# Expert weights in pairs: full-precision matmuls on column tiles, 2 MB loads for two experts

## What is computed

```
def _expert_choice_moe(xn, w_router, w_gate, w_up, w_down):
    cap = EC_FACTOR * n_tok // N_EXPERTS           # 64 latent, 16 context
    aff = jax.nn.softmax(jnp.dot(xt, w_router), axis=-1)
    g, idx = lax.top_k(aff.T, cap)
    xe = xt[idx]
    h = jax.nn.silu(einsum('ecd,edf->ecf', xe, w_gate)) * einsum('ecd,edf->ecf', xe, w_up)
    ye = einsum('ecf,efd->ecd', h, w_down) * g[..., None]
    out = jnp.zeros_like(xt).at[idx.reshape(-1)].add(ye.reshape(-1, D))
```

## Time and profile before

| | us |
|---|---|
| median of three runs | 2026.26 |
| profiled execution | 2036.07 |
| its span, first to last instruction | 2034.3 |
| PE busy | 1811.8 (89%) |
| VectorE busy | 1511.7 (74%) |
| ScalarE busy | 1144.3 (56%) |
| GpSimd busy | 527.7 (26%) |
| weight loads busy (PEld) | 1273.2 (63%) |

### The profile page before, as it was taken

The page is one execution under the profiler, slowest core; times in us unless marked ns, Lnnn a source line. Parts: engine busy times, 40 slices in busy tenths (PEclk is TensorE's granted clock), DMA queues, the critical chain, the costliest instruction groups (busy, mean ns, idle before and its releaser), DMA issues.

```text
span 2034.3 us, 24624 instructions
## 1 busy us (share of the span) xinstructions
PE 1811.8 (89%) x8919; PEld 1273.2 (63%) x8919; DVE 1511.7 (74%) x1438; ACT 1144.3 (56%) x1134; POOL 527.7 (26%) x320
## 2 busy tenths in 40 slices
PE   5899789699999999999478799898699999999995
PEld 2788567366666666665257588777466666666663
DVE  2477553599999999998255466635799999999994
ACT  2477621277777777775231235412477777777773
POOL 1223210214343433331210320000123334343332
PEclk8899887699999999999788779796799999999997
DMA  9300726699999999999730510007499999999992
GB/s 387 104 1 1 279 104 234 259 347 379 382 367 380 364 383 368 380 387 345 96 131 1 191 63 2 1 1 303 159 362 374 379 383 368 380 368 383 366 387 61
DMA packets 139901, 519.03 MB, mean 255 GB/s; under 512 B 14943, under 2 KB 15231, under 8 KB 138814
## 3 DMA queue, kind: packets, MB, share of 16 engines
q1 hardware_dynamic: 131248, 488.02, 62.7%
q0 software_dynamic: 7216, 24.79, 6.3%
q10 hardware_dynamic: 1374, 5.37, 0.6%
HBM read 496.90 MB, written 21.24 MB: 255 GB/s over the span
## 4 chain that ended last, share of the span: by engine, by line
PE 65%; DVE 15%; issue 7%; ACT 6%; DMA 4%; SPq 1%; POOL 1%; DVEq 0%; POOLq 0%; ACTq 0%
PE ps L783 25%; PE ps L788 14%; DVE whl L1536 7%; PE ps L739 6%; PE ps L988 4%; ACT whl L1158 3%; PE ps L1035 2%; DMA ring<-in_at_w_qkv 2%; PE ps L1008 2%; PE ps L1024 2%; DMA ring<-in_mod_w 2%; PE ps L719 1%; DVE W L1554 1%; PE ps L892 1%; SPq L353 1%
## 5 line engine op out<-in xcount | busy, mean ns | idle before, releaser
L1536 DVE TENSOR_TENSOR whl<-ring,whl 128x2048 fp32r<-128x2048 f32 x384 | 922.8, 2428 | 84.8 <-ACT whl L1158 81.6
L1158 ACT ACTIVATE whl<-ring 128x2048 fp32r<-128x2048 f32 x384 | 735.8, 1917 | 247.4 <-PE ps L788 247.1
L783 PE MATMUL ps<-whl,xs_hl 128*80 128x512 f32 x2048 | 558.8, 395 | 8.3 <-DVE xs_hl L1560 4.8
L783 PEld LDWEIGHTS ps<-whl,xs_hl 128*80 128x80 f32 x2048 | 299.5, 149 | 168.0 <-issue 7.0
L788 PE MATMUL ps<-whl,xs_hl 128*80 128x512 f32 x1024 | 322.4, 396 | 19.0 <-DVE whl L1536 19.0
L783 PE MATMUL ps<-whl,hs_hl 128*80 128x512 f32 x1024 | 280.8, 396 | 3.4 <-ACT hs_hl L1065 3.4
L788 PEld LDWEIGHTS ps<-whl,xs_hl 128*80 128x80 f32 x1024 | 147.7, 148 | 117.4 <-DVE whl L1536 41.9
L580 POOL TENSOR_TENSOR W<-W 80x1024 f32<-80x1024 f32 x32 | 89.9, 2808 | 495.5 <-ACT W L1196 495.5
L783 PEld LDWEIGHTS ps<-whl,hs_hl 128*80 128x80 f32 x1024 | 153.3, 150 | 89.1 <-ACT hs_hl L1065 3.6
L788 PE MATMUL ps<-whl,hs_hl 128*80 128x512 f32 x512 | 160.8, 396 | 0.0
L574 POOL COPY sg<-g_t 80x1 f32 (+1 forms) x32 | 82.7, 2585 | 189.8 <-DMA x_mid<-W,si 99.1
(11 more groups left out here) (253 smaller groups left out, 2481.9 us busy)
## 6 DMA issues: line engine op xcount, KB each, us to landing
ring<-in_moe_w_gate SPq DMA_DIRECT2D x128, 1024.0 KB, 8.0
ring<-in_moe_w_up SPq DMA_DIRECT2D x128, 1024.0 KB, 7.2
ring<-in_moe_w_down SPq DMA_DIRECT2D x128, 1024.0 KB, 7.2
ring<-in_mod_w SPq DMA_DIRECT2D x48, 1024.0 KB, 9.8
ring<-in_rg_w_in SPq DMA_DIRECT2D x8, 1024.0 KB, 21.9
ring<-in_at_w_qkv SPq DMA_DIRECT2D x8, 768.0 KB, 20.3
x_hat<-r ACTq DMA_DIRECT2D x2, 2560.0 KB, 19.0
ring<-in_rg_w_out SPq DMA_DIRECT2D x4, 1024.0 KB, 9.6
```

Source lines behind the costliest of these rows:

```text
L783: nc.tensor.matmul(ps[0:CE, bank + n, :], xhl[:, part, k, :], w[:, 0, n * 512:(n + 1) * 512], start=(k == 0 and part == 0), stop=False)
L1158: nc.scalar.activation(whl[:, whl_slot(u), 0, :], ring[:, slot, :], ACT.Copy).then_inc(whi_ok, 1)
L1536: v.tensor_tensor(whl[:, whl_slot(u), 1, :], ring[:, n % MSLOTS, :], whl[:, whl_slot(u), 0, :].bitcast(F32), ALU.subtract).then_inc(wlo_ok, 1)
```

## The change

- Experts are worked on in pairs (8 pairs in a layer). No weight is split: the matmuls take float32 operands. For a contraction block and a half of the columns, expert a's 64 latent rows are the stationary operand of a matmul into PSUM partitions 64a to 64a+63, so that the two experts stand on two column tiles; the 16 context rows of two experts and two halves are four matmuls into partitions 0, 32, 64 and 96.
- All 12 slots hold raw weights. The host lays the weights out so that one load of 2 MB brings two contraction blocks of both experts into two neighbouring slots, with 16 KB of one piece for each partition. A load waits for the matmuls that used its slots (`moe_used`).
- x of a pair is gathered by two indirect DMAs (128 latent rows, 48 rows with the context's), turned and modulated in two parts; scale and shift are taken from the mod vectors by broadcast. The router's indices and weights are kept in pair form (ten small copies).
- VectorE alone forms the output (one operation for 128 latent rows, four for the context), and GpSimd scatters in two rounds of two DMAs, the second behind the landing of the first.
- `mod_w`, `rg_w_out` and `at_w_o` are laid out by the host with 8 KB of one piece per partition and slot; gains, rotary table and sinks come ready from the host in 3 loads instead of 5.
- Half of the qkv loads go out behind mod vectors 9 and 10 as slots come free, the other half when vector 10 has been used; none waits for `x_mid`. The first four blocks are split before it.

The core of the diff:

```diff
+                def part(slot, w, i, s):
+                    sp.dma_start(ring[:, slot:slot + 2, :].rearrange("p (o a) n -> p o (a n)", o=1),
+                                 w3[w][:, bass.ds(i * 4 + s, 1), :]).then_inc(slot_ready[slot], 16)
...
+                def step_loads(i, par, more, _):
+                    for n in range(0, 24 if more else 8, 2):
+                        what = n // 8 if more else 1
+                        sp.wait_ge(moe_used, i * PAIR_USES + (LAYER_USES * layer + n // 2 + 3))
+                        part(n % SLOTS, (0, 2, 1)[what], i + int(what != 1), n % 8 // 2)
...
+            load_mod(9, moe_used, lambda s: LAYER_USES - 6 + s // 2 + 1)
+            load_mod(10, moe_used, lambda s: LAYER_USES - 4 + s // 2 + 1)
...
+            for s in range(4, KB):
+                sp.wait_ge(moe_used, LAYER_USES - 4 + s // 2 + 1)
+                load_qkv(s)
+            for s in range(4):
+                sp.wait_ge(ring_used, used(10, s))
+                load_qkv(s)
...
+                    if rows_left:
+                        next_rows(i + 2)
+                    pool.wait_ge(ob_ok, i * 5 + (41 * layer + 1 + 5))
+                    pool.wait_ge(sg_ok, i * 4 + 4 * (pb + 1))
+                    for a in range(2):
+                        passed()
+                        scatter(si_l[:, a:a + 1], ob_l[a * CL:(a + 1) * CL, :])
+                        scatter(si_c[:, a:a + 1], ob_c[a * CG:a * CG + CC, :])
+                        pool.wait_ge(scattered, i * 64 + (64 * pb + 32 * (a + 1)))
...
+                def product(n0, ready_at, bank, lat, ctx):
+                    for s in range(4):
+                        slots = [(n0 + 2 * s + a) % SLOTS for a in range(2)]
+                        pe.wait_ge(slot_ready[slots[0]], ready_at(n0 + 2 * s))
+                        for h in range(2):
+                            k = 2 * s + h
+                            for n in range(2):
+                                cols = slice(h * D + n * 512, h * D + (n + 1) * 512)
+                                for a in range(2):
+                                    nc.tensor.matmul(ps[a * CL:(a + 1) * CL, bank + n, :], lat(a, k), ring[:, slots[a], cols],
+                                                     start=(k == 0), stop=(k == KB - 1))
+                            for q in range(4):
+                                a, n = q // 2, q % 2
+                                mm = nc.tensor.matmul(ps[q * CG:q * CG + CC, bank + 2, :], ctx(a, k),
+                                                      ring[:, slots[a], h * D + n * 512:h * D + (n + 1) * 512],
+                                                      start=(k == 0), stop=(k == KB - 1))
+                        mm.then_inc(moe_used, 1)
+                        yield s
...
+                    if more:
+                        pe.wait_ge(xt_ok, i * 2 + 2 * (pb + 2))
+                        pe.wait_ge(ob_ok, i * 5 + (41 * layer + 1))
+                        pe.wait_ge(sil_ok, i * 2 + 2 * (pb + 1))
+                        for s in gate_up(0, at, x, 1 - par):
+                            if s < 2:
+                                h_turn(i, s)
...
+                    pe.wait_ge(ht_ok, i * 2 + 2 * (pb + 1))
+                    for s in down(8 if more else 0, at, y):
+                        if s < 3 and rows_left:
+                            x_turn(i + 2, s)
...
+def pair_rows(w):
+    w = slot_rows(w)
+    return w.reshape(2, NP, 2, 4, P, 2 * D).transpose(0, 1, 3, 4, 2, 5).reshape(2, NP * 4, P, 4 * D)
```

More of the change, by code:

```diff
@@ L198, in build @@
         xn2 = work(5 * D, 0)
[L199 to L205, removed]
+        xt = work(2 * KB * XW, 0).rearrange("p (u k n) -> p u k n", u=2, k=KB)
+        ht_l = work(D).rearrange("p (k n) -> p k n", k=KB)
+        ht_c = work(512).rearrange("p (k n) -> p k n", k=4)
+        xg_l = work(D, 5 * D)
+        hs_l = work(D)
+        hs_c = work(512)
+        work(512)
+        xg_c = work(D)
+        ob_l = work(D)
+        ob_c = work(D)
+        gg_l = work(D)
+        gg_c = work(512)
         tk = work(512)
@@ L272, in runs, with loads_before, ready, used @@
             return out
[L277 to L303, removed]
+        def loads_before(name, slot):
+            n = 0
+            for what in SLOT_LOADS[slot // 4]:
+                if what == name:
+                    return n
+                if what in ("moe0", "moe1"):
+                    n += 0 if slot % 2 else SLOT_USES
+                else:
+                    n += 1
+        def ready(name, slot):
+            return 16 * (loads_before(name, slot) + 1)
+        def used(v, s):
+            return 4 * MOD_ORDER.index(v) + s % 4 + 1
+        def first_ready(layer, n):
+            return 16 * (loads_before(f"moe{layer}", n % SLOTS) + (n - 8) // SLOTS + 1)
+        def body_ready(layer, i, n):
+            return i * 32 + 16 * (loads_before(f"moe{layer}", n % SLOTS) + (1 if n % SLOTS < 8 else 2) + n // SLOTS + 1)
         def steps(eng, body):
-            with eng.Fori(0, NE // 2 - 1) as i:
+            with eng.Fori(0, NP // 2 - 1) as j:
                 for par in range(2):
-                    body(i * 2 + par, i, par, True, True)
-            body(NE - 2, NE // 2 - 1, 0, True, False)
-            body(NE - 1, NE // 2 - 1, 1, False, False)
+                    body(j * 2 + par, par, True, True)
+            body(NP - 2, 0, True, False)
+            body(NP - 1, 1, False, False)
         x_tiles = x_all.rearrange("(t p) d -> p t d", p=P)
@@ L355, in pair @@
[L355 to L365, removed]
@@ L367, in load_moe, with put @@
-            def load_moe(layer):
[L368 to L376, removed]
+            def put(slot, src):
+                sp.dma_start(ring[:, slot, :], src).then_inc(slot_ready[slot], 16)
@@ L377, in load_moe @@
                     else:
                         sp.wait_ge(out_mm, 2 * NT)
[L379 to L389, removed]
+                    part(slot, int(n >= 16), 0, n % 8 // 2)
@@ L856, in experts @@
+                at = lambda n: first_ready(layer, n)
+                pe.wait_ge(gg_ok, 2 * (layer + 1))
+                x_turn(0, 0)
+                x_turn(0, 1)
+                x_turn(0, 2)
+                pe.wait_ge(ob_ok, 41 * layer + 1)
+                pe.wait_ge(xt_ok, 2 * (pb + 1))
+                for s in gate_up(8, at, 0, 0):
+                    if s < 3:
+                        x_turn(1, s)
+                for _ in gate_up(16, at, 3, 0):
+                    pass
                 steps(pe, body)
```

599 lines of the change are left out of this document (262 added, 337 removed).

## The result

| | before | after |
|---|---|---|
| median of the runs, us | 2028.54 (5 runs, 2024.73 to 2031.66) | 2046.26 (5 runs, 2039.47 to 2050.68) |
| ratio after to before | | 1.0087, 95% interval 1.0062 to 1.0112 |
| profiled execution's span, us | 2034.3 | 2048.9 |
| PE busy | 1811.8 (89%) | 1843.4 (90%) |
| VectorE busy | 1511.7 (74%) | 606.5 (30%) |

The split went, VectorE and ScalarE were relieved as forecast, and the kernel became 0.9% slower. The forecast was 1883. From the page of the kernel after: busy time by engine, the slices of PE, VectorE and DMA, the packets, and the two groups of expert matmuls (busy us, mean ns, idle time before them and its releaser).

What follows compares the result with a forecast made beforehand. PE was taken as today's bound, with DMA (65.2 us a pair) replacing it after the change. Terms -77 - 77 + 2 - 1 + 9 + 0 = -144, scaled to -143, gave 1883 us, range 1850 to 2000.

Steps and rivals of the forecast that it cites:

- the price of a full-precision matmul: On PE in the expert stages: 0.43 us per matmul of 512 columns, so 1.28 us a block and 30.7 a pair.
- Overlap of the tiles: Expert matmuls on PE: tiles of 64 columns and of 32 both overlap fully, 30.7 us a pair before transposes.
- tiles don't overlap: Rival for the expert matmuls: 89 us a pair on PE, 2315 us; chance 0.05 together with the low clock.
- Changes of width: Between latent and context matmuls on PE: 48 changes a pair at 0.16 us, 8 us, making PE 46 instead of 38.
- Transposes: Turning x and the hidden rows on PE: 28 transposes at 0.25 us, 7 us a pair.
- DMA: Expert loads of 2 MB with 16 KB rows: 32.6 us per expert, 65.2 per pair, taking PE's place as bound.
- Prefetch: Expert stages: 12 MB ready or under way at the first product instead of 8; 494 against 571 us, -77 per layer.
- End: After the last expert matmul: five VectorE operations and two rounds of scatters, +9 us.
- After layer 0: From layer 0's last expert matmul to the qkv product: later x_mid against no qkv wait; nothing, give or take 10 us.
- Start: At the kernel's start: twelve mod loads go from 4 KB to 8 KB rows, -1 us.
- The indirect loop: Rival in the expert stages: gathers and scatters become the bound; 75 us a pair gives 1951, past 83 slower, chance 0.07.
- The lower clock: Rival on PE: clock 0.50 throughout gives 77 to 90 us a pair, 2070 to 2200; chance 0.05 together with no overlap.

Runs made afterwards that it cites:

- e5: Kernel after with each latent matmul made as two on 32-column tiles, so no tile width changes inside a product: 1976.94 us, 0.973 of before.
- e1: Kernel after without the latent matmuls of the pair's second expert, one of the two 64-column tiles: 2043.51 us, 1.0049 of before.
- e4: Kernel after with the latent matmuls of a load's two blocks first, then the context matmuls of both: 1995.19 us, 0.9802 of before.
- e8: e5 with PE's loop over pairs written out, so PE has no branch back: 1953.15 us, 0.9622 of before.
- e2: Kernel after with all context matmuls of the experts left out: 1890.29 us, 0.9296 of before.
- e6: e2 with each 2 MB load split into two of 1 MB with 8 KB in a row: 1896.08 us, 0.9334 of before.
- e7: Kernel after, nothing left out, with each 2 MB load split into two of 1 MB with 8 KB in a row: 2060.12 us, 1.0154 of before.

## Why the prediction failed, step by step

**The step that failed: the price of a full-precision matmul.** "A full-precision matmul of 512 columns: four back to back took 1.88 us, 0.43 each". The four were four instructions of the profile. In the code of before, `gate_rows` makes 4 matmuls at L694 in each of its two calls, 8 in all, and the profile has 16; `modulation` makes 4 for each of 4 slots of 12 vectors, 192, and the page of the kernel before counts 384:

```profile
L679 PE MATMUL ps<-ring,cond 128*2 128x512 f32 x384 | 57.3, 725 | 14.0 <-DMA ring<-in_mod_w 12.6
```

The "32 in 3.61 us" of the earlier trace rows are 16 matmuls of the program in four groups of four: 0.86 a group, not 0.43. I divided by the profile's count and multiplied by the program's. With 0.86 the same working gives 24 x 3 x 0.86 = 61.9 for the products, 7 for the transposes (measured 3.3, see below) and 48 x 0.16 = 7.7 for the changes of width: 77, or 69 without the changes. Both are over DMA's 65.2. It would have said: PE stays the bound, at the 70.5 of before or slower, no gain.

The Trainium skill's page "FP8 and Floating Point Precision" (TensorE Precision Notes) says that true FP32 takes four passes through the PE array. The rows agree: four passes of 512 columns at 2.4 GHz would be 0.853 us, an estimate from that page's figure, and a round measures 0.86 (e5) at the granted clock of 1.00 (2.4 GHz).

Before, a split product (three fp32r matmuls at 0.24) was 0.72. So a block of a pair, transposes spread over it, went from 4 x 0.72 = 2.88 us to 71.65 / 24 = 2.99: the context's 16 rows, which used to ride along with the latent rows, are a round of their own now, and the widths change.

**Overlap of the tiles: right.** Full overlap for both widths (e1 for 64 columns, L789's groups of four on 32). The rival "tiles don't overlap" is out. But the sign that the prediction had named for it, 0.85 us for a group of two latent matmuls, did appear: at the doubled price it is the sign of full overlap, and only e1 tells the two apart.

**Changes of width: right in size, wrong in weight.** I estimated 0.16 us each; e4 gives 0.14, and the difference between a block of the kernel after and one of e5, 2.85 - 2.575 = 0.275, is two of them. The Trainium skill's page "TensorEngine Tiling (Array Packing)" (Key Properties) says that a change of tiling mode drains the array; the trace agrees in so far as every change costs this 0.14 us. I put the 8 us a pair aside as "still below what follows". On a PE that is the bound they are 24 x 0.275 = 6.6 us a pair; e8, which avoids them, has pairs that are 6.0 us shorter (65.6 against 71.65).

**Transposes: too high, by the clock of the row.** A pair's cost besides its blocks is 71.65 - 24 x 2.85 = 3.3 us, half of my 7. The row that I read, eight in 1.97 us, lies in a stretch of the kernel before at a granted clock of 0.50 (1.2 GHz). In the experts of the kernel after, at 1.00, eight take 1.09 with the tail:

```profile
1141.30:1143.30 2.00, 1.97 (x8) 1.57 (x8) 0.00 (x0) 0.00 (x0) 0.75 (x2) 0.50 1.00 406
...
542.20 1.09 PE L812 MATMUL ps<-ident,W 128*128 128x128 f32 x8
```

Transposes appear once each (code line 812 makes 8 a pair, and 16 pairs give the x128 of the profile), so the factor of two is not in them.

**DMA: right, but not the bound.** 65.2 a pair forecast; in e2 64.5 by the gate loads. The parts were off by a little and in part cancel: over one pair of e2 (570 to 634.4 us) the weights' queue has a share of 93.0% and the indirect queue 8.1%, thus 59.9 and 5.2 us where I had 61.4 and 5.6; together they read 1.011, where I divided by the 1.026 of 4 KB packets. The packet sum holds: with 16 KB packets and next to nothing beside them the queue moves the 429 GB/s that it gave (e2, layer 0):

```profile
424.00:440.00 16.00, 15.68 (x78) 5.60 (x76) 1.82 (x2) 1.62 (x2) 0.00 (x0) 1.00 1.01 429
```

With 8 KB packets it is 421 (e6, 422 to 438 us). Beside gathers and scatters the size was worth 0.8 us a pair where I took 1.0 (e6).

**Prefetch: right where DMA paces.** 494 us per layer forecast, 493.7 and 494.3 in e2. That it fits this closely is luck: the pairs are 0.8 us shorter than my 65.2, 6 us over 7.5 of them, and what a layer takes beside them is 10.7 us instead of my 5.2. In the kernel after it has no part, since no load is waited for.

**End: right.** +9 forecast, +9.9 measured. The chain that ended last in the kernel after (start, length, what) shows the output's passes and the second round behind the landing of the first:

```profile
2022.32 1.03 PE ps L789 x8
...
2023.37 1.28 DVE W L1524
...
2028.46 1.45 POOL out_y_all L553
2030.22 3.68 DMA out_y_all<-W,si_c
2034.69 1.41 POOL out_y_all L553
2036.41 1.30 POOL out_y_all L553
```

**After layer 0: inside its bounds.** I had 0, give or take 10, from the last matmul to the qkv product; it is 59.6 us before and 53.6 after, -6. The scatters come back later, and the wait for qkv weights is gone, as forecast; `x_mid` is back 33 us after the last matmul, where I had 40:

```profile
977.84 8.73 DMA x_mid<-W,si_c
...
989.06 3.64 DMA x_mid<-W,si_c
...
993.00 10.20 DMA r<-x_mid
...
1023.50 34.52 PE ps L1005 x144
```

**Layer 1's start and the stages between: not resolved.** The stretch between the expert stages is 0.6 us shorter, the 6 won behind layer 0 lost again before layer 1. Kernels with the same code there lie between 468.7 and 482.2 there, so terms of 2 us can't be read from one profile each.

**Start: larger than forecast.** -8.6 against -1; among the variants -4 to -8.6. The 8 KB rows of the mod loads account for 1 by my sum; where the rest comes from was not tested.

**The rivals.** The indirect loop never became the bound: PE waits for a gather once, 8.6 us ahead of layer 1's first products, and the scatters landed in 9.0 us at the median, at most 10.0, beside 16 KB packets, against 8.4 and 11.3 before. The lower clock didn't decide either: within the pairs PE never waits, and its clock is 1.00, as that rival itself had said of a PE without waits. Its premise, that waiting for loads brings the lower clock, isn't borne out in e2 (0.98), and its 2070 to 2200 us don't follow from 77 to 90 us a pair: by the prediction's own 7.5 pairs a layer, 90 would be 1883 + 2 x 7.5 x 24.8 = 2255. The outcome, slower, was among my cases with 0.12, for other reasons; that PE simply stays the bound because a price is double was not among them.

## What to carry to other kernels

Before a duration from the profile becomes a price per instruction, count the program's instructions in the loop and compare with the count in the row; where they differ by a factor of two, divide the time by the program's. Look at the granted clock of the row's stretch as well. Trading a three-pass split for full-precision matmuls took work off VectorE and ScalarE but not off PE, and here it paid only once the changes of tile width were fewer (e4, matmuls of one width grouped: 2% faster than before) or gone (e5 and e8, one width throughout: 2.7 and 3.8%). The larger load was worth something where the loads were waited for (e2 against e6).

## What the runs showed of the hardware

- A full-precision matmul of 512 columns takes 0.86 us at a granted clock of 1.00 and appears as two instructions 0.43 apart; two on tiles of 64 columns (e1), or four on tiles of 32 (e5), take as long as one. A transpose of 128 columns appears once.
- Going from one tile width to the other and back costs 0.275 us, 0.14 each way (e4, e5).
- PE's branch back in a loop cost 3.6 to 4.2 us in e5 and in layer 1 of e7, where the loop's instructions were loaded again (11 and 9 packets a round), and nothing that shows in layer 0 of e7, in the kernel after or, written out straight, in e8. Behind such a gap the granted clock was 0.50, which cost another 2 to 3 us.
- The weights' queue moved 429 GB/s with 16 KB packets (e2), next to 410 and 422 with 4 and 8 KB. Beside gathers and scatters, 16 KB instead of 8 KB shortened a pair by 0.8 us of 65 (e2 against e6).
